# Third block's output projection: the stream's eight residual adds on GpSimd, placed between its weight splits, in place of VectorE

## The chip, the cores and the metric

The kernel runs on one core of a Trainium2 chip. The metric is the device time of one execution in microseconds (us). The core's engines are TensorE (PE, with its weight loads shown as PEld), VectorE (DVE), ScalarE (ACT), GpSimd (POOL) and SyncE (SP), which issues the weight loads from DRAM. Each engine runs its own instructions in program order, and they meet at semaphores.

## The reference, cut to what matters

Three blocks run one after the other on a stream of 1024 positions and 1024 features. The change lies in the third block, at the step that is marked:

```python
y = jnp.concatenate([rmsnorm_3(y_lru, out_norm_lru_g[l]),
                     rmsnorm_3(y_cc, out_norm_cc_g[l])], axis=-1)
h = h + y @ w_out[l].astype(y.dtype)                                  # this step

m = rmsnorm_3(h, norm_mlp_g[l]) @ w_mlp_up[l].astype(h.dtype)
h = h + jnp.square(jax.nn.relu(m)) @ w_mlp_down[l].astype(h.dtype)
```

## The kernel before

The stream `H3` lies in SBUF with features on the partitions, as eight tiles (index `b`) of 128 features x 1024 positions in float32. Every matrix product is made of three: each float32 operand is split into a high part and a low part (`whi`, `wlo` for weights, `xhi`, `xlo` for data), and PE multiplies high by high, high by low and low by high.

**Weights.** They come as slots of 16 tiles of 128x128. SP loads a slot into `RAW`, and GpSimd splits it (`split`, four pieces of 128x512, each a high part at L573 or L575 and a low part at L577) into one of two buffers. PE gives a buffer back when it starts the slot after it (`slot_used`), so GpSimd can be one slot ahead of PE. In a part of the third block ScalarE makes the high parts (`weights_high`), and GpSimd makes the low ones only (`split_low`, L585); the last slot made so is the second and last one of `out_3b`. The slot after it is the first of the MLP's up projection (`up_3_0`), the next one its second.

**The projection.** `w_out` is applied in two halves. The half over the recurrent branch (`out_3a`) has been added to the stream's old value by then, and lies in `HL3`, two tiles named `h3_low` (b 0 to 3) and `h3_high` (b 4 to 7). The half over the convolution branch, `out_3b`, is multiplied out by `feature_tiles` into PSUM, eight outputs in four "quads" of two; a quad's half of PSUM is used again two quads later. Its result needs a factor per position, `INVC` (`cc_inverse`). So for each of the eight outputs VectorE does two things: L2702 multiplies the PSUM result by `INVC` into `H3[b]` and frees its part of PSUM, and L2704 adds `HL3` to it and counts up `h3_done`.

**What follows.** After `h3_done` ScalarE squares the tile (`norm_square`, L302) for the sum of the next norm, and makes its high part with the norm's gain (`raw_high`, L342). VectorE adds up the squares (`norm_add`, L310) and makes the low part (`raw_low`, L346). These stand in one written order on each engine. On VectorE it is: multiply and add for b, then the norm's add and the low part for b-1, up to b = 4; at b = 5 the norm's adds for 4 and 5 and the low parts of 4 and 5; then multiply and add of 6 and 7, the low parts of 6 and 7, and the norm's adds of 6 and 7. On ScalarE it is square and high part of 0, 1, 2, 3, then squares of 4 and 5, high parts of 4 to 7, squares of 6 and 7.

The up projection's first output multiplies all eight tiles in order (k = 0 to 7) and waits before each one for its low part. The norm's factor itself is not needed then: its column sums are taken (L323) in the second output, and it is applied to the results.

Of the kernel before, what the change touches and what calls it, by code (L numbers as in the profile page):

```python
# [26 lines left out]
P = 128  # L27
D = 1024
KB = D // P
T = 1024  # L30
# [140 lines left out]
def build(nc, xT, memT, stream, params, wqkv, sgu, bias2, lru_w, metaT, outT, o_scr, h_scr, blocks=(1, 2, 3)):  # L171
    TL, WH = plan(blocks)
    NSLOT = len(TL) // TILES
    with ExitStack() as ctx:
# [15 lines left out]
        def L(name, n):  # L190
            return S(name), LATER[name][1] + n
# [5 lines left out]
        def S(name):  # L197
            if name in LATER:
                name = LATER[name][0]
            if name not in sems:  # L200
                sems[name] = ctx.enter_context(nc.semaphore(name))
            return sems[name]
# [3 lines left out]
        def at(name, offset, shape, dt=F32):  # L206
            return nc.alloc_sbuf_tensor_at(name, shape, dt, offset=base + offset)
# [12 lines left out]
        A = C + 8512  # L220
# [23 lines left out]
        def free(quad):  # L244
            return S(f"quad_free{quad % 2}")

        def freed(quad, ob, loop=None):

            return up(2 * (quad // 2) + ob + 1, loop)
# [4 lines left out]
        SHARED_3 = range(WH["vg_1"][0], WH["up_3_0"][0])  # L254
        SHARED = [*SHARED_M, *SHARED_3]
# [271 lines left out]
        if 1 in blocks:  # L527
            XS = at("x_in", A, [P, KB, T])
            MS = at("mem_in", A + 72704, [P, KB, MEM])

        def load_input(queue, b):
            queue.dma_start(XS[:, b:b + 2, :], xT[P * b:P * (b + 2), :].rearrange("(b p) t -> p b t", p=P))\
# [2 lines left out]
        def load_memory(queue, b):  # L535
            queue.dma_start(MS[:, b:b + 4, :], memT[P * b:P * (b + 4), :].rearrange("(b p) t -> p b t", p=P))\
                .then_inc(S("mem_moved"), 16)
# [25 lines left out]
        @block.gpsimd  # L563
        def _(pool):
            def split(r, loads, done, used):
                pool.wait_ge(raw_loaded[r], loads)
                if used is not None:
                    pool.wait_ge(slot_used, used)
                for piece in range(PIECES_W):
                    t = slice(TILES // PIECES_W * piece, TILES // PIECES_W * (piece + 1))  # L570
                    if piece == 0:
                        one = par("ones", 0, P).unsqueeze(1).to_broadcast([P, TILES // PIECES_W, P])
                        nc.gpsimd.tensor_tensor(WHI[:, r, t], RAW[:, r, t], one, ALU.mult).then_inc(hi_done, 1)  # L573
                    else:
                        nc.gpsimd.tensor_copy(WHI[:, r, t], RAW[:, r, t]).then_inc(hi_done, 1)  # L575
                    pool.wait_ge(hi_done, done + piece + 1)
                    ins = nc.gpsimd.tensor_tensor(WLO[:, r, t], RAW[:, r, t], WHI[:, r, t].bitcast(F32), ALU.subtract)  # L577
                ins.then_inc(split_done, 1)

            def split_low(s):  # L580
                r = s % 2
                for piece in range(PIECES_W):
                    t = slice(TILES // PIECES_W * piece, TILES // PIECES_W * (piece + 1))
                    pool.wait_ge(S("hi_by_act"), 2 * SHARED.index(s) + 2 * piece // PIECES_W + 1)
                    ins = nc.gpsimd.tensor_tensor(WLO[:, r, t], RAW[:, r, t], WHI[:, r, t].bitcast(F32), ALU.subtract)  # L585
                ins.then_inc(split_done, 1)

            def splits(first, end, fewer):
                if first % 2 and first < end:
                    split(1, 16 * (first // 2 + 1), PIECES_W * (first - fewer), first - 1)  # L590
                    first += 1
                if first // 2 < end // 2:
                    with pool.Fori(first // 2, end // 2) as i:
                        for r in range(2):
                            split(r, i * 16 + 16, i * (2 * PIECES_W) + PIECES_W * (r - fewer), i * 2 + (r - 1))
                if end % 2:
                    split(0, 16 * (end // 2 + 1), PIECES_W * (end - 1 - fewer), end - 2)

            for s in SHARED_M:
                split_low(s)  # L600
            pool.wait_ge(S("par_loaded"), 16)
            splits(SHARED_M.stop, SHARED_3.start, len(SHARED_M))
            for s in SHARED_3:
                split_low(s)
            splits(SHARED_3.stop, NSLOT, len(SHARED))


        if 1 in blocks:
# [50 lines left out]
            MXL = at("mem_lo", A + 65536, [P, KB, MEM], F32R)  # L659
            NRMM = norm_set("nm", lambda b: MS[:, b, :], MEM, lambda b: par("mem_norm_g", b), A + 81920, WH["mem_k"][1],  # L660
                            hi=lambda b: MXH[:, b, :], lo=lambda b: MXL[:, b, :])
# [887 lines left out]
        if 2 in blocks:  # L1549
# [15 lines left out]
                         at=NRM2["bank"] + 2 * BANK, columns=NRM2["bank"] + 2 * BANK, names=("e_sq", "e_add", "e_step", "e_x"))  # L1565
# [394 lines left out]
        if 3 in blocks:  # L1960
# [122 lines left out]
            SQ3 = at("squares_3", A, [P, 2, T])  # L2083
            DIAG3 = at("diag_3", A + 8192, [P, T])
            DIAG3M = at("diag_mean_3", A + 12288, [P, T])
            HL3 = [at("h3_low", A + 66624, [P, 4, T]), at("h3_high", A + 33536, [P, 4, T])]
            INVC = at("cc_inverse", A + 50240, [P, T])
            ROWS3 = at("rows_3", A + 83264, [64, T])
            THIRDS = ((0, 348), (348, 346), (694, 346))
# [1 line left out]
            MCOL = small("cc_mean_columns", [P, NT])  # L2091
            VCOL = small("cc_var_columns", [P, NT])
            RCOL = small("cc_root_columns", [P, NT])
            H3 = at("h3", A, [P, KB, T])
            NRMP = norm_set("n3p", lambda b: H3[:, b, :], T, lambda b: par("norm_mlp_g_3", b), A + 54336, WH["up_3_0"][1],
                            hi=lambda b: XHI[:, b, :], lo=lambda b: XLO[:, b, :], bank=2, spread_at=A + 81920)
            NRME = norm_set("n3o", lambda b: H3[:, b, :], T, lambda b: par("norm_final_g_3", b), A + 32768, 0,
# [75 lines left out]
        def pe_block3(pe):  # L2173
# [67 lines left out]
            def lru_half(o, between=None):  # L2241
# [22 lines left out]
                for a in (0, HALF):  # L2264
                    mm = nc.tensor.matmul(ps[:, c0 + a:c0 + a + HALF], IDENT, HL3[o // 4][:, o % 4, a:a + HALF],
                                          start=False, stop=True)
# [41 lines left out]
        def act_block3(act):  # L2308
# [130 lines left out]
            act.wait_ge(S("l_scan"), 4)  # L2439
            act.dma_start(HL3[0][:, :, :], h_blocks[:, 0:4, :]).then_inc(S("h3_loaded0"), 16)  # L2440
            act.wait_ge(S("cc_conv"), 2 * (CCK - 1))
# [18 lines left out]
            act.wait_ge(*L("l_lo", 4))  # L2460
            act.dma_start(HL3[1][:, :, :], h_blocks[:, 4:8, :]).then_inc(S("h3_loaded1"), 16)

# [70 lines left out]
        def dve_block3(dve):  # L2533
# [165 lines left out]
            for b in range(KB):  # L2699
                q = WH["out_3b"][1] + b // 2  # L2700
                dve.wait_ge(quad_ready, q + 1)
                nc.vector.tensor_tensor(H3[:, b, :], half(q, b % 2), INVC[:, :], ALU.mult).then_inc(free(q), 1)  # L2702
                dve.wait_ge(free(q), freed(q, b % 2))
                nc.vector.tensor_tensor(H3[:, b, :], H3[:, b, :], HL3[b // 4][:, b % 4, :], ALU.add).then_inc(S("h3_done"), 1)  # L2704
                if 1 <= b < 6:
                    norm_add(dve, NRMP, b - 1)
                if 1 <= b < 5:
                    raw_low(dve, NRMP, b - 1)
                if b == 5:
                    norm_add(dve, NRMP, 5)  # L2710
                    raw_low(dve, NRMP, 4)
                    raw_low(dve, NRMP, 5)
# [116 lines left out]
```

## Time and profile before

| | before |
|---|---|
| median of 3 runs | 3512.65 us (3509.48 to 3513.63) |
| the profiled execution | 3508.49 us, its span 3506.7 us |
| PE busy | 3337.4 us, 95% |
| DVE busy | 1362.1 us, 39% |
| POOL busy | 1194.7 us, 34% |
| ACT busy | 760.3 us, 22% |
| chain that ended last | PE 87%, DVE 8%, ACT 3% |

PE is busy nearly all of the time, so the kernel's time moves only where PE waits, or where it does its work at a lower clock. The stretch that matters here lies between 2736 and 2801 us from the start of the span: `out_3b`, and the first outputs of the up projection behind it. The views used are the page's lines on busy time and on the chain, the chain of waits in that stretch, and the timelines of single engines in it. In a timeline a row gives the start, the duration, the engine, the line and operation, what is written and read, and in brackets the engine's idle time before it and what ended that.

### The profile page before, as it was taken

The page shows a single profiled execution, that of the slowest core. Times are in us where ns is not written, and L with a number is a line of the kernel's source. Part 1 is how long each engine was busy: PE and PEld are TensorE (multiplying, and loading weights), DVE is VectorE, ACT ScalarE, POOL GpSimd, SP SyncE. Part 2 cuts the span into 40 slices and gives each one's busy share as a digit, 9 for nine tenths or more (in the row PEclk, how much of TensorE's full clock was granted, in tenths as well). Part 3 has the DMA queues.
Part 4 walks back from the last instruction along what each step waited for, and adds up shares of the span by engine and source line. Part 5 has one row for each costly group of instructions (what it writes and reads, how often), then busy time and mean ns, then how long its engine had stood idle before and what let it go on. Part 6 is the DMA issues. An engine that isn't in the chain of part 4 may idle for free.

```text
span 3506.7 us, 37515 instructions
## 1 busy us (share of the span) xinstructions
PE 3337.4 (95%) x15576; PEld 2680.3 (76%) x15576; DVE 1362.1 (39%) x1653; ACT 760.3 (22%) x1108; POOL 1194.7 (34%) x992
## 2 busy tenths in 40 slices
PE   7999989999898999999999999998998999999997
PEld 6577767888785788888888888887965788888886
DVE  6264073331505402233331111238997652222223
ACT  4220164221205401112100000023542310000001
POOL 5212300354330233344443433342321454444441
PEclk9989999999898999999999999998998999999998
DMA  4111100021210011121111111112111111111111
GB/s 186 37 43 43 49 1 25 25 89 65 105 48 13 24 48 55 43 97 48 48 49 48 48 48 48 48 48 78 37 60 48 36 49 48 48 48 48 48 48 48
DMA packets 32333, 181.72 MB, mean 52 GB/s; under 512 B 3920, under 2 KB 4944, under 8 KB 15312
## 3 DMA queue, kind: packets, MB, share of 16 engines
q1 hardware_dynamic: 19936, 139.99, 11.2%
q10 hardware_dynamic: 12272, 39.89, 3.0%
q8 instruction: 99, 1.62, 0.2%
q14 instruction: 26, 0.21, 0.0%
HBM read 164.15 MB, written 15.73 MB: 51 GB/s over the span
## 4 chain that ended last, share of the span: by engine, by line
PE 87%; DVE 8%; ACT 3%; issue 1%; POOL 1%; DMA 0%; DVEq 0%; ACTq 0%; SPq 0%; POOLq 0%
PE ps L451 50%; PE ps L485 17%; PE ps L2134 5%; PE ps L516 4%; DVE c_out L2584 2%; PE ps L1635 1%; PE ps L860 1%; PE ps L1651 1%; PE ps L2156 1%; PE ps L733 1%; PE ps L2210 1%; DVE p L1830 1%; PE ps L1621 1%; PE ps L742 1%; PE ps L877 1%
## 5 line engine op out<-in xcount | busy, mean ns | idle before, releaser
L573 POOL TENSOR_TENSOR whi<-raw,par 128x512 fp32r<-128x512 f32 x116 | 127.8, 1102 | 1923.7 <-PE ps L451 1398.3
L577 POOL TENSOR_TENSOR wlo<-raw,whi 128x512 fp32r<-128x512 f32 x464 | 687.5, 1482 | 37.0
L451 PE MATMUL ps<-xhi,whi 128*128 128x512 f32 x2016 | 628.0, 393 | 11.8 <-DVE xlo L346 4.3
L451 PE MATMUL ps<-xlo,whi 128*128 128x512 f32 x2016 | 624.1, 391 | 0.0
L451 PE MATMUL ps<-xhi,wlo 128*128 128x512 f32 x2016 | 622.7, 390 | 0.0
L451 PEld LDWEIGHTS ps<-xhi,whi 128*128 128x128 f32 x2016 | 376.9, 188 | 95.5 <-issue 5.3
L451 PEld LDWEIGHTS ps<-xhi,wlo 128*128 128x128 f32 x2016 | 379.7, 188 | 81.0
L451 PEld LDWEIGHTS ps<-xlo,whi 128*128 128x128 f32 x2016 | 380.0, 189 | 80.3
L575 POOL CAST whi<-raw 128x512 fp32r<-128x512 f32 x348 | 287.8, 827 | 0.0
L485 PE MATMUL ps<-hidden_hi,whi 128*128 128x512 f32 x864 | 268.6, 392 | 0.4 <-DVE hidden_lo L1491 0.4
L485 PE MATMUL ps<-hidden_lo,whi 128*128 128x512 f32 x864 | 268.9, 393 | 0.0
L485 PE MATMUL ps<-hidden_hi,wlo 128*128 128x512 f32 x864 | 267.1, 390 | 0.0
L1506 DVE TENSOR_TENSOR h<-h,ps 128x1024 f32<-128x1024 f32 x112 | 132.3, 1217 | 337.7 <-PE ps L485 337.7
L1453 ACT ACTIVATE ff_act<-ps 128x1024 f32<-128x1024 f32 x46 | 47.3, 1028 | 977.3 <-PE ps L451 977.3
L585 POOL TENSOR_TENSOR wlo<-raw,whi 128x512 fp32r<-128x512 f32 x60 | 110.7, 1874 | 290.0 <-ACT whi L262 290.0
L485 PEld LDWEIGHTS ps<-hidden_hi,wlo 128*128 128x128 f32 x864 | 162.2, 188 | 36.7
L485 PEld LDWEIGHTS ps<-hidden_lo,whi 128*128 128x128 f32 x864 | 162.3, 188 | 35.7
L485 PEld LDWEIGHTS ps<-hidden_hi,whi 128*128 128x128 f32 x864 | 161.3, 188 | 36.4 <-issue 1.7
L2584 DVE SCALAR_TENSOR_TENSOR c_out<-c_in,par,c_out 128x1024 f32<-128x1024 f32 x120 | 179.2, 1495 | 4.9 <-ACT c_out L2356 1.4
L1482 DVE TENSOR_TENSOR ff_tmp<-ff_act,ps 128x1024 f32<-128x1024 f32 x18 | 22.0, 1221 | 328.0 <-ACT ff_act L1453 328.0
L1487 DVE TENSOR_TENSOR ff_tmp<-ff_act 128x1024 f32<-128x1024 f32 x32 | 41.7, 1303 | 216.6 <-ACT ff_act L1453 216.5
L1491 DVE TENSOR_TENSOR hidden_lo<-ff_tmp,hidden_hi 128x1024 fp32r<-128x1024 f32 x54 | 90.6, 1678 | 63.9 <-ACT hidden_hi L1456 63.9
(487 smaller groups left out, 4577.3 us busy)
## 6 DMA issues: line engine op xcount, KB each, us to landing
raw<-stream SPq DMA_DIRECT2D x131, 1024.0 KB, 4.7
x_again<-xT ACTq DMA_DIRECT2D x4, 1024.0 KB, 8.0
h_scr<-x_again ACTq DMA_DIRECT2D x4, 1024.0 KB, 4.4
h<-h_scr ACTq DMA_DIRECT2D x1, 4096.0 KB, 15.4
h_scr<-h ACTq DMA_DIRECT2D x4, 1024.0 KB, 4.6
outT<-h ACTq DMA_DIRECT2D x8, 512.0 KB, 3.0
bias<-bias ACTq DMA_DIRECT2D x1, 2560.0 KB, 9.0
x_in<-xT ACTq DMA_DIRECT2D x2, 1024.0 KB, 17.5
```

The lines of the kernel that those rows point to most:

```text
L451: mm = nc.tensor.matmul(ps[:, c0 + c:c0 + c + width], w, x(k, a, width), start=(n == 0 and m == 0), stop=(n == len(ks) - 1 and m == 2))
L485: mm = nc.tensor.matmul(ps[:, c0 + c:c0 + c + HALF], w, x(k, a, HALF), start=(k == 0 and m == 0), stop=(k == n - 1 and m == 2))
L516: mm = nc.tensor.matmul(ps[:, c:c + BANK], x(k, P * tt, P), w, start=(k == 0 and m == 0), stop=(k == KB - 1 and m == 2))
L573: nc.gpsimd.tensor_tensor(WHI[:, r, t], RAW[:, r, t], one, ALU.mult).then_inc(hi_done, 1)
L575: nc.gpsimd.tensor_copy(WHI[:, r, t], RAW[:, r, t]).then_inc(hi_done, 1)
L577: ins = nc.gpsimd.tensor_tensor(WLO[:, r, t], RAW[:, r, t], WHI[:, r, t].bitcast(F32), ALU.subtract)
L585: ins = nc.gpsimd.tensor_tensor(WLO[:, r, t], RAW[:, r, t], WHI[:, r, t].bitcast(F32), ALU.subtract)
L1453: nc.scalar.activation(FA[:, j % 2, :], half(q, 0), ACT.Silu if k == "f2" else ACT.Relu)\
L1491: nc.vector.tensor_tensor(HL[:, j, :], FT[:, j % 2, :], HH[:, j, :].bitcast(F32), ALU.subtract)\
L1506: nc.vector.tensor_tensor(stream_tile[:, b, :], stream_tile[:, b, :], half(q, b % 2), ALU.add).then_inc(free(q), 1)
L2134: mm = nc.tensor.matmul(ps[:, c0 + BANK * i:c0 + BANK * i + width], w, x(k, a, width), start=(k == 0 and m == 0), stop=(k == KB - 1 and m ...
L2584: nc.vector.scalar_tensor_tensor(CCO[:, b, :], CC[:, b, META + k:META + k + T], par("cc_conv_w_3", 4 * k + b), CCO[:, b, :], ALU.mult, ALU ...
```

## The change

VectorE keeps the eight multiplications by `INVC` and loses the eight adds of `HL3`. GpSimd gets them, as a function `residual(b)`: it waits for VectorE's multiplication of b, for the load of `HL3` and for ScalarE's last write to it, adds 128x1024 values and counts up `h3_done`. In GpSimd's order the adds of b = 0, 1, 2 stand behind the last `split_low`, then comes the split of the up projection's first slot, then the adds of b = 3 to 7, then the remaining splits.

```diff
+            def residual(b):
+
+                q = WH["out_3b"][1] + b // 2
+                pool.wait_ge(free(q), freed(q, b % 2))
+                pool.wait_ge(*L(f"h3_loaded{b // 4}", 16))
+                pool.wait_ge(*L("lh_kept", 8))
+                nc.gpsimd.tensor_tensor(H3[:, b, :], H3[:, b, :], HL3[b // 4][:, b % 4, :], ALU.add).then_inc(S("h3_done"), 1)
+
+            s = SHARED_3.stop
+            for b in range(3):
+                residual(b)
+            splits(s, s + 1, len(SHARED))
+            for b in range(3, KB):
+                residual(b)
+            splits(s + 1, NSLOT, len(SHARED))
-            splits(SHARED_3.stop, NSLOT, len(SHARED))
...
                 nc.vector.tensor_tensor(H3[:, b, :], half(q, b % 2), INVC[:, :], ALU.mult).then_inc(free(q), 1)
-                dve.wait_ge(free(q), freed(q, b % 2))
-                nc.vector.tensor_tensor(H3[:, b, :], H3[:, b, :], HL3[b // 4][:, b % 4, :], ALU.add).then_inc(S("h3_done"), 1)
```

GpSimd's order behind the last `split_low` (40 subtractions in a row), before. `raw` is the loaded slot, `num_ready` stands for `lh_kept`, `x_again0` and `x_again1` for the loads of `HL3`, `quad_free` for VectorE's multiplication:

```order
53 L585 TENSOR_TENSOR wlo<-raw,whi 128x512 [waits hi_by_act] x40
54 L573 TENSOR_TENSOR whi<-raw,par 128x512 [waits slot_used,raw_loaded1]
55 L577 TENSOR_TENSOR wlo<-raw,whi 128x512 [waits hi_done]
56 L575 CAST whi<-raw 128x512
57 L577 TENSOR_TENSOR wlo<-raw,whi 128x512 [waits hi_done]
58 L575 CAST whi<-raw 128x512
```

and in the changed kernel, where `h_61` is the stream `H3`:

```order
53 L587 TENSOR_TENSOR wlo<-raw,whi 128x512 [waits hi_by_act] x40
54 L614 TENSOR_TENSOR h_61<-h_61,h_low 128x1024 [waits num_ready,x_again0,quad_free0] x2
55 L614 TENSOR_TENSOR h_61<-h_61,h_low 128x1024 [waits num_ready,x_again0,quad_free1]
56 L575 TENSOR_TENSOR whi<-raw,par 128x512 [waits slot_used,raw_loaded1]
...
63 L579 TENSOR_TENSOR wlo<-raw,whi 128x512 [waits hi_done]
64 L614 TENSOR_TENSOR h_61<-h_61,h_low 128x1024 [waits num_ready,x_again0,quad_free1]
65 L614 TENSOR_TENSOR h_61<-h_61,h_high 128x1024 [waits num_ready,x_again1,quad_free0] x2
66 L614 TENSOR_TENSOR h_61<-h_61,h_high 128x1024 [waits num_ready,x_again1,quad_free1] x2
```

The eight adds stand in front of and behind the split of the first up slot, and the next split stands behind them all.

VectorE's order from the multiplication of b = 5 on, before:

```order
1132 L2702 TENSOR_TENSOR h3_535<-ps,cc_inverse_529 128x1024 [waits quad_ready]
1133 L2704 TENSOR_TENSOR h3_535<-h3_535,h3_high_528 128x1024 [waits quad_free0]
1134 L310 TENSOR_TENSOR n3p_acc_537<-n3p_acc_537,n3p_sq_536 128x1024 [waits norm_add,norm_sq] x2
1135 L346 SCALAR_TENSOR_TENSOR xlo_53<-h3_535,par_54,xhi_52 128x1024 [waits norm_hi] x2
1136 L2702 TENSOR_TENSOR h3_535<-ps,cc_inverse_529 128x1024 [waits quad_ready]
1137 L2704 TENSOR_TENSOR h3_535<-h3_535,h3_high_528 128x1024 [waits quad_free1]
1138 L2702 TENSOR_TENSOR h3_535<-ps,cc_inverse_529 128x1024 [waits quad_ready]
1139 L2704 TENSOR_TENSOR h3_535<-h3_535,h3_high_528 128x1024 [waits quad_free1]
1140 L346 SCALAR_TENSOR_TENSOR xlo_53<-h3_535,par_54,xhi_52 128x1024 [waits norm_hi] x2
```

and in the changed kernel:

```order
1127 L2717 TENSOR_TENSOR h3_61<-ps,cc_inverse_562 128x1024 [waits quad_ready]
1128 L310 TENSOR_TENSOR n3p_acc_569<-n3p_acc_569,n3p_sq_568 128x1024 [waits norm_add,norm_sq] x2
1129 L346 SCALAR_TENSOR_TENSOR xlo_53<-h3_61,par_54,xhi_52 128x1024 [waits norm_hi] x2
1130 L2717 TENSOR_TENSOR h3_61<-ps,cc_inverse_562 128x1024 [waits quad_ready] x2
1131 L346 SCALAR_TENSOR_TENSOR xlo_53<-h3_61,par_54,xhi_52 128x1024 [waits norm_hi] x2
```

Only the adds are gone; the multiplications of 6 and 7 still stand behind the norm's add of 5 and the low parts of 4 and 5.

## Rows read from the trace of the kernel before

**Rows 1.** The page: busy time of each engine, and the chain by engine.

```profile
PE 3337.4 (95%) x15576; PEld 2680.3 (76%) x15576; DVE 1362.1 (39%) x1653; ACT 760.3 (22%) x1108; POOL 1194.7 (34%) x992
PE 87%; DVE 8%; ACT 3%; issue 1%; POOL 1%; DMA 0%; DVEq 0%; ACTq 0%; SPq 0%; POOLq 0%
```

**Rows 2.** The chain of waits, 2736 to 2830: start, us, engine and line.

```profile
2736.29 10.95 PE ps L451 x48
...
2747.26 1.24 DVE h L2702
...
2779.80 1.56 DVE xlo L346
2781.36 0.04 issue
2781.40 6.02 PE ps L451 x18
```

**Rows 3.** Timeline of PE, the end of six steps and the next two.

```profile
2768.82 0.62 PE L451 MATMUL ps<-xhi,whi 128*128 128x512 f32 x2
...
2776.52 0.61 PE L451 MATMUL ps<-xhi,wlo 128*128 128x512 f32 x2
2781.40 0.85 PE L451 MATMUL ps<-xhi,whi 128*128 128x512 f32 x2 [4.26 <-DVE xlo L346]
...
2783.75 1.10 PE L451 MATMUL ps<-xhi,whi 128*128 128x512 f32 x2
...
2787.26 1.84 PE L323 MATMUL ps<-par,n3p_acc 128*128 128x1 f32 x16
```

**Rows 4.** Timeline of DVE, 2737 to 2784.

```profile
2737.39 1.23 DVE L2702 TENSOR_TENSOR h<-ps,cc_inverse 128x1024 f32<-128x1024 f32 x1 [4.29 <-ACT cc_inverse L2499]
2738.65 2.11 DVE L2704 TENSOR_TENSOR h<-h,h_low 128x1024 f32<-128x1024 f32 x1
...
2744.18 2.31 DVE L346 SCALAR_TENSOR_TENSOR xlo<-h,par,xhi 128x1024 fp32r<-128x1024 f32 x1
2747.26 1.23 DVE L2702 TENSOR_TENSOR h<-ps,cc_inverse 128x1024 f32<-128x1024 f32 x1 [0.77 <-PE ps L451]
2748.52 1.25 DVE L2704 TENSOR_TENSOR h<-h,h_low 128x1024 f32<-128x1024 f32 x1
...
2762.44 1.22 DVE L310 TENSOR_TENSOR n3p_acc<-n3p_acc,n3p_sq 128x1024 f32<-128x1024 f32 x1
2763.58 1.28 DVE L346 SCALAR_TENSOR_TENSOR xlo<-h,par,xhi 128x1024 fp32r<-128x1024 f32 x1
2764.77 1.22 DVE L2702 TENSOR_TENSOR h<-ps,cc_inverse 128x1024 f32<-128x1024 f32 x1
...
2779.72 3.85 DVE L346 SCALAR_TENSOR_TENSOR xlo<-h,par,xhi 128x1024 fp32r<-128x1024 f32 x2
```

**Rows 5.** Timeline of ACT, square and high part of tile 0.

```profile
2740.79 1.06 ACT L302 ACTIVATE n3p_acc<-h 128x1024 f32<-128x1024 f32 x1 [1.54 <-DVE h L2704]
2741.75 1.14 ACT L342 ACTIVATE xhi<-h,par 128x1024 fp32r<-128x1024 f32 x1
```

**Rows 6.** Timeline of POOL, 2738 to 2801.

```profile
2738.38 7.04 POOL L585 TENSOR_TENSOR wlo<-raw,whi 128x512 fp32r<-128x512 f32 x4 [70.11 <-ACT whi L262]
2747.59 1.09 POOL L573 TENSOR_TENSOR whi<-raw,par 128x512 fp32r<-128x512 f32 x1 [2.18 <-PE ps L451]
...
2759.13 2.15 POOL L577 TENSOR_TENSOR wlo<-raw,whi 128x512 fp32r<-128x512 f32 x1
2769.29 1.38 POOL L573 TENSOR_TENSOR whi<-raw,par 128x512 fp32r<-128x512 f32 x1 [8.01 <-PE ps L451]
...
2800.93 1.16 POOL L573 TENSOR_TENSOR whi<-raw,par 128x512 fp32r<-128x512 f32 x1 [18.44 <-PE ps L451]
```

**Rows 7.** Timeline of POOL from 3304 on, a split in the MLP.

```profile
3304.41 1.09 POOL L573 TENSOR_TENSOR whi<-raw,par 128x512 fp32r<-128x512 f32 x1 [13.65 <-PE ps L451]
3305.58 1.29 POOL L577 TENSOR_TENSOR wlo<-raw,whi 128x512 fp32r<-128x512 f32 x1
3306.82 0.61 POOL L575 CAST whi<-raw 128x512 fp32r<-128x512 f32 x1
...
3311.36 1.28 POOL L577 TENSOR_TENSOR wlo<-raw,whi 128x512 fp32r<-128x512 f32 x1
```

## What was predicted before the changed kernel ran

> **What bounds the kernel now.** I read the page first: PE is busy 95% of the span and carries 87% of the chain [rows 1], so only what delays PE counts. The chain of waits in the stretch of the projection comes second. It leaves PE at 2747.26, when the third and fourth outputs are multiplied out, goes through VectorE's list of work without a break, and comes back to PE at 2781.40 [rows 2]. The timeline of PE shows the price: the up projection's first output starts at 2768.82, does six of its eight steps by 2777.1, and idles 4.26 us for the low part of tile 6 [rows 3]. Then the two steps from 2781.40 to 2785.88 take 4.5 us, where six took 8.3 us, so 1.37 us each: another 1.7 us are lost to slow matmuls after the gap. Taking this stall away whole would give 4.3 + 1.7 = 6 us. The event to follow is the low part of tile 7, done at 2783.57 [rows 4]; PE starts its eighth step at 2783.75 [rows 3].
>
> **What things take.** VectorE's multiplication takes 1.23 us, a two-input operation without disturbance 1.2 [rows 4]; ScalarE's square 1.06 and high part 1.14 us [rows 5]. VectorE's operations with two inputs in SBUF are stretched where GpSimd works: the add at 2738.65 took 2.11 and the low part at 2744.18 took 2.31 us, against 1.25 and 1.28 at other places [rows 4], and GpSimd's subtraction 2.15 against 1.29 us [rows 6, 7]. The stretch of 1.1 us is one instruction of the other engine: they take turns. The multiplication reads PSUM and one SBUF tile, and isn't stretched.
>
> GpSimd has no 128x1024 operation in the trace. The nearest is its subtraction of 128x512, 1.29 us, with the next instruction 1.24 us behind it [rows 7]. Twice the spacing is 2.48 us; a fixed part that is paid once rather than twice makes it less, and turn-taking makes it more. I take 2.45 us. The bounds are 2.2 (0.25 us of fixed part) and, if an add is disturbed for its whole length as the worst subtractions are, 2 x 2.15 = 4.3 us [rows 6].
>
> The Trainium skill (GPSIMD Engine Reference, section 3.1) gives 4497 ns for an add of 2048 columns against 2293 ns on VectorE. Half of it would be an estimate of 2.25 us, and the sum below would come out at +5 in place of +7 us. The subtraction of 512 columns, 1.29 us, is a little above a quarter of it (1.12), so the trace bears it out with a fixed part of some 0.15 us.
>
> **The walk through the changed kernel.** Adds on GpSimd are A0 to A7.
>
> The last `split_low` holds GpSimd from 2738.38 for 7.04 us, with three turns lost to VectorE's adds and a low part [rows 6]; the adds are gone and the low part comes later, so four spacings of 1.24 end it at 2743.3. Before, add 0 was done at 2740.8. Now A0 ends at 2745.7 and A1 at 2748.1. Square and high part of tile 0 end at 2747.9, its low part at 2749.2, and only behind it stands the multiplication of tile 2, done 2750.3. The norm's add 1 takes the turn to 2751.4, so A2 ends at 2753.8. The split of the first up slot, which began at 2747.59 [rows 6], begins behind A2: 6.2 us late. A split by itself takes 8.2 us (3304.41 to 3312.64) [rows 7]; this one took 13.7 (2747.59 to 2761.28) [rows 6]. Now only the low parts of 1 and 2 and the norm's add 2 take turns with it, 1.0 us each, so it ends near 2765.1, 3.8 us later than now; PE doesn't want it before 2768.82.
>
> But tile 3 has to wait for it: A3 runs to 2767.5, A4 to 2769.9. On VectorE the norm's add 3 and low part 3 (high part 3 at 2769.7) stand ahead of multiplication 5, which ends at 2773.3 in place of 2766 [rows 4]. PE needs that PSUM at 2768.82 for its first up output, so it starts 4.5 us late; six steps end by 2781.6, and even with 1.7 us for slow matmuls by 2783.3. A5 loses a turn to the norm's add 4 and ends at 2776.7. Square 5, high part 4 and high part 5 on ScalarE (3.2 us) end at 2779.9, low parts 4 and 5 at 2781.4, and behind them multiplication 6 at 2782.6. A6 ends at 2785.1, A7 at 2787.5, high part 7 at 2788.7. Low part 6 has waited for A7's turn and ends at 2788.7; GpSimd's next split takes a turn of 1.1, and low part 7 ends at 2790.8. That is 7.2 us behind the 2783.57 of now. Walking the kernel of before in the same way ends 0.1 to 0.7 us later than its trace, so I take 7 us.
>
> The gap of PE ahead of its seventh step grows to some 5 us, at 1.7 us of slow matmuls as now. The norm's add 7 ends at 2794.7; PE wants it for the column sums at the same time, 3.5 us after its eighth step began, as now (2783.75 to 2787.26) [rows 3], so it adds nothing. The second up slot, split from 2769.29 on before [rows 6], is split from 2787.5, with two low parts and two adds in its way, to 2799.6; PE took it up at 2800.9, where GpSimd's next split was released [rows 6], and now does at 2807.9. That cover of 8 us hides it. The load of slots by SP hangs on splits and stays ahead. The rest of the MLP is PE work and moves as a whole.
>
> Sum: eight VectorE adds gone, which would be worth up to 6 us at PE; in their place eight adds of twice the length, one of which stands behind a split of 11 us, and hand-overs from VectorE to GpSimd to ScalarE and back that VectorE's own order makes serial. +7 us. Each 0.1 us of GpSimd's add moves it by 0.75 us, as seven to eight adds lie on this path: 2.2 gives +5, 2.6 gives +8. The profiled execution was 3508.5 and would be 3515.5; it lies 4.2 us below the median of the runs. The median, 3512.65, plus 7 gives **3519.6 us**.
>
> **The rule of turns.** The rows show turns of 1.1 us only. The Trainium skill (SBUF — State Buffer, section Who interferes with whom) says that a VectorE instruction with two SBUF inputs and a GpSimd instruction that reads SBUF exclude each other for the whole instruction, whoever comes first. By that rule an add of 2.45 us makes VectorE wait up to 2.3 us, which the walk has in it at low parts 1 and 6 and at add 3. If a long add let VectorE in, those waits and what they push would go, and the walk would end about 4 us sooner, at +3. No row has so long an instruction on GpSimd.
>
> **Rivals.**
> 1. *Nearly hidden.* The wide add is at its lower bound, or VectorE isn't held for the whole of it: +2 to +5 us. For it: PE's gap was 4.3 us, so the path has been off PE's own work for long only from tile 4 on. Against it: the walk's turns all have a pattern in rows 4 and 6. Chance 0.27.
> 2. *GpSimd's add is dearer*, 3 us or more, through turns lost within it or slower dispatch: at 3 us +11, at 4.3 us +21 or so, where the second up slot's split also has its cover used up to the last microsecond. It decides from 2.6 us on. Chance 0.17.
> 3. *Faster.* VectorE's list was the bound from 2747 to 2781, and eight of its operations, 1.25 to 2.11 us each [rows 4], 10 to 17 us together, leave it. If GpSimd worked beside it freely, PE would find all low parts in time: at most 6 us less, 3506.6. The mechanism needs an add at 1.3 us or less, or no turns at all; then the walk ends level with now. Against it stands that multiplications 5 and 6 each wait on VectorE behind work that needs the add before. Chance 0.05.
> 4. *The change doesn't do what it says:* VectorE isn't relieved, as it stands idle where it was busy. This is in the forecast, and has no time of its own.
>
> **How the numbers follow.** Forecast, +5 to +10 us, 0.51; rival 1, 0.27; rival 2, 0.17; rival 3, 0.05. A measurement of this kernel tells 0.2%, 7 us, from no change. The forecast's own case lies astride that bound and gives 0.33 to slower and 0.18 to the same; rival 1 is the same, rival 2 slower, rival 3 faster. That makes faster 0.04, same 0.46, slower 0.50. The range leaves out the far part of rival 2 and rival 3: +1.4 to +14 us, 3514 to 3526.5.
>
> **What would show it.** In the timeline of GpSimd: adds near 2.45 us, and add 3 beginning some 11 us after add 2 ended. In VectorE's: idle times ended by ScalarE where there were none, and multiplications 5 and 6 about 7 us later. On PE: a new wait of about 4 us ahead of the first up output, ended by VectorE's multiplication, and a wait of about 5 us ahead of the seventh step. The prediction is wrong if the split of the first up slot ends before 2762, if the adds take under 2 or over 2.8 us, or if PE's column sums start less than 3 us later than 2787.3.

## The result, and the profile after

| | before | after |
|---|---|---|
| median | 3510.12 us (20 runs, 3507.37 to 3515.4) | 3516.4 us (20 runs, 3514.12 to 3522.09) |
| ratio to before | | 1.0018, 95% interval 1.0012 to 1.0024 |
| span of the profiled execution | 3506.7 us | 3514.6 us |
| DVE busy | 1362.1 us | 1350.1 us |
| POOL busy | 1194.7 us | 1210.7 us |

The changed kernel is 6.3 us slower by the medians. That is just inside the 0.2% that was set as the limit of no change, and the interval of the ratio, 4.2 to 8.4 us, lies wholly above zero. The first three runs of the kernel before had a median 2.5 us above that of all its 20 runs, so 2.5 of the 3.2 us between the forecast of 3519.6 and the measured 3516.4 lie in the starting point.

The page of the changed kernel, busy time and the chain by engine (compare [rows 1]):

```profile
PE 3340.9 (95%) x15576; PEld 2681.2 (76%) x15576; DVE 1350.1 (38%) x1645; ACT 761.9 (22%) x1108; POOL 1210.7 (34%) x1000
PE 86%; DVE 8%; ACT 3%; issue 2%; POOL 1%; DMA 0%; DVEq 0%; ACTq 0%; SPq 0%; POOLq 0%
```

Times inside the stretch can be compared from one common point, ScalarE's copy of `INVC` ahead of VectorE's first multiplication. It starts at 2736.33 us before and at 2737.13 after; the 0.8 us between them arose earlier, in code that is the same. GpSimd in the changed kernel (compare [rows 6]; L614 is the add, L575 to L579 the split):

```profile
2739.19 5.05 POOL L587 TENSOR_TENSOR wlo<-raw,whi 128x512 fp32r<-128x512 f32 x4 [71.61 <-ACT whi L262]
2744.19 4.79 POOL L614 TENSOR_TENSOR h<-h,h_low 128x1024 f32<-128x1024 f32 x2
2751.28 3.33 POOL L614 TENSOR_TENSOR h<-h,h_low 128x1024 f32<-128x1024 f32 x1 [2.29 <-DVE h L2717]
2754.56 2.08 POOL L575 TENSOR_TENSOR whi<-raw,par 128x512 fp32r<-128x512 f32 x1
...
2765.84 2.42 POOL L614 TENSOR_TENSOR h<-h,h_low 128x1024 f32<-128x1024 f32 x1
2768.22 2.38 POOL L614 TENSOR_TENSOR h<-h,h_high 128x1024 f32<-128x1024 f32 x1
2774.09 3.29 POOL L614 TENSOR_TENSOR h<-h,h_high 128x1024 f32<-128x1024 f32 x1 [3.49 <-DVE h L2717]
2783.33 4.69 POOL L614 TENSOR_TENSOR h<-h,h_high 128x1024 f32<-128x1024 f32 x2 [5.95 <-DVE h L2717]
2787.97 2.08 POOL L575 TENSOR_TENSOR whi<-raw,par 128x512 fp32r<-128x512 f32 x1
...
2808.73 1.16 POOL L575 TENSOR_TENSOR whi<-raw,par 128x512 fp32r<-128x512 f32 x1 [7.86 <-PE ps L451]
```

An undisturbed add takes 2.4 us. Add 3 starts at 2765.84, 11.2 us after add 2 ended, since the split stands between them. Three times GpSimd waits for VectorE's multiplication, 2.29, 3.49 and 5.95 us, and all three times VectorE's order has the multiplication behind work that needs an earlier add. VectorE, in the same stretch (compare [rows 4]):

```profile
2738.19 2.36 DVE L2717 TENSOR_TENSOR h<-ps,cc_inverse 128x1024 f32<-128x1024 f32 x2 [4.30 <-ACT cc_inverse L2514]
2748.77 1.30 DVE L346 SCALAR_TENSOR_TENSOR xlo<-h,par,xhi 128x1024 fp32r<-128x1024 f32 x1 [8.22 <-ACT xhi L342]
...
2752.26 3.43 DVE L346 SCALAR_TENSOR_TENSOR xlo<-h,par,xhi 128x1024 fp32r<-128x1024 f32 x1
...
2769.39 2.29 DVE L310 TENSOR_TENSOR n3p_acc<-n3p_acc,n3p_sq 128x1024 f32<-128x1024 f32 x1 [8.07 <-ACT n3p_sq L302]
...
2772.80 1.21 DVE L2717 TENSOR_TENSOR h<-ps,cc_inverse 128x1024 f32<-128x1024 f32 x1
...
2786.93 4.20 DVE L346 SCALAR_TENSOR_TENSOR xlo<-h,par,xhi 128x1024 fp32r<-128x1024 f32 x2 [2.55 <-ACT xhi L342]
```

VectorE, which hardly stood still before, is idle for 8.22 and 8.07 us, and its last low part ends at 2791.13, 54.0 us after the common point where it was 47.2 (2783.57 less 2736.33). The wait on PE, which is what counts (compare [rows 3]; the second row shown here is the seventh step, the third the column sums):

```profile
2774.07 1.22 PE L451 MATMUL ps<-xhi,whi 128*128 128x512 f32 x2 [4.28 <-DVE h L2717]
...
2789.15 0.89 PE L451 MATMUL ps<-xhi,whi 128*128 128x512 f32 x2 [4.20 <-DVE xlo L346]
...
2794.98 1.93 PE L323 MATMUL ps<-par,n3p_acc 128*128 128x1 f32 x16
```

There is a new wait of 4.28 us ahead of the first up output, and the old one ahead of the seventh step is still 4.20 us long. Behind each wait the matmuls are slow for a while: a pair takes 1.05 us where 0.62 is usual, and the clock granted to PE is 0.50 of full speed (1.2 GHz) from 2775 to 2778 us and from 2790 to 2792, where it is 1.00 (2.4 GHz) from 2784 to 2788. Before, it was 0.50 from 2782 to 2784, behind the one wait.

### The profile page after: what moved, and what is told of

Same layout as the page of the kernel before. It is cut to its first block, busy times and chain, and to the rows that moved or that the text cites. A ratio compares the mean times of both kernels' runs of the same rounds, so it can differ in the third digit from the quotient of the medians.

```text
span 3514.6 us, 37523 instructions
## 1 busy us (share of the span) xinstructions
PE 3340.9 (95%) x15576; PEld 2681.2 (76%) x15576; DVE 1350.1 (38%) x1645; ACT 761.9 (22%) x1108; POOL 1210.7 (34%) x1000
## 4 chain that ended last, share of the span: by engine, by line
PE 86%; DVE 8%; ACT 3%; issue 2%; POOL 1%; DMA 0%; DVEq 0%; ACTq 0%; SPq 0%; POOLq 0%
PE ps L451 50%; PE ps L485 17%; PE ps L2149 5%; PE ps L516 4%; DVE c_out L2599 2%; PE ps L877 1%; PE ps L1652 1%; PE ps L1668 1%; PE ps L750 1%; PE ps L2225 1%; DVE p L1847 1%; PE ps L759 1%; PE ps L1638 1%; POOL h L614 1%; PE ps L894 1%
## 5 line engine op out<-in xcount | busy, mean ns | idle before, releaser
L575 POOL TENSOR_TENSOR whi<-raw,par 128x512 fp32r<-128x512 f32 x116 | 129.6, 1117 | 1903.9 <-PE ps L451 1375.0
L579 POOL TENSOR_TENSOR wlo<-raw,whi 128x512 fp32r<-128x512 f32 x464 | 685.0, 1476 | 36.9
```

## The experiments

Beside the medians, the table gives a local figure: the time from the common point to PE's start on the second up slot, which is where GpSimd's following split is released (2800.93 in [rows 6]). It is read in the one profiled execution and is free of what happens elsewhere in the 3500 us. For the kernel before it is 64.6 us. How much it varies from one execution to the next wasn't measured; two pairs of kernels that should differ little there, before and e9, after and e7, agree within 0.1 us.

| kernel | median, us | before in the same comparison | ratio, 95% interval | local, us | against before |
|---|---|---|---|---|---|
| after | 3516.4 | 3510.12 | 1.0018 (1.0012 to 1.0024) | 71.6 | +7.0 |
| e1 all adds ahead of the split | 3530.26 | 3510.01 | 1.0059 (1.0042 to 1.0076) | 85.5 | +20.9 |
| e2 half of each add | 3510.14 | 3510.01 | 1.0002 (0.9993 to 1.0012) | 65.1 | +0.5 |
| e3 each add in two halves | 3517.24 | 3510.01 | 1.0021 (1.0011 to 1.0031) | 72.4 | +7.8 |
| e4 adds 3 to 7 on GpSimd | 3511.25 | 3510.01 | 1.0007 (0.9998 to 1.0017) | 67.5 | +2.9 |
| e5 split held back, before | 3506.86 | 3509.57 | 0.9994 (0.9985 to 1.0003) | 61.7 | -2.9 |
| e6 no adds | 3505.55 | 3509.57 | 0.9987 (0.9978 to 0.9996) | 58.4 | -6.2 |
| e7 split held back, after | 3516.3 | 3509.57 | 1.0019 (1.001 to 1.0029) | 71.5 | +6.9 |
| e8 held back, and reordered | 3504.23 | 3509.64 | 0.9983 (0.9974 to 0.9992) | 59.5 | -5.1 |
| e9 reordered only | 3510.05 | 3509.64 | 1.0001 (0.9991 to 1.001) | 64.5 | -0.1 |
| e10 held back until add 7 | 3505.09 | 3509.64 | 0.9987 (0.9977 to 0.9996) | 59.7 | -4.9 |

The theory was that of the prediction: the adds' length on the path, and the split that stands between add 2 and add 3 (theory A). Its main rival was that the hand-overs between three engines cost the time, whatever is handed over (theory B).

### e1: all eight adds ahead of the first up slot's split

```diff
-            for b in range(3):
+            for b in range(KB):
                 residual(b)
-            splits(s, s + 1, len(SHARED))
-            for b in range(3, KB):
-                residual(b)
-            splits(s + 1, NSLOT, len(SHARED))
+            splits(s, NSLOT, len(SHARED))
```

> All eight adds stand on GpSimd in front of the first up slot's split, nothing is left out. Theory A (the path runs through eight wide adds, and the split between them holds adds 3 to 7 back by 11 us): without the split in between, the low part of tile 7 is done about as early as in the kernel before, within 2 us of it (some 46 us after VectorE's first multiplication, where the changed kernel has 53). But PE then waits for the split itself, which ends near 28 us after the adds began to end: PE's first up output starts some 24 us later than before, and the time is 3530 us, 20 us over the kernel before. Theory B (the hand-overs between the three engines cost the time, wherever the split stands): the low part of tile 7 stays 6 to 7 us late and the time is 3536 us, 26 over the kernel before.

Measured: 3530.26 us. GpSimd's timeline, the last adds and the split that PE now waits for:

```profile
2756.74 3.31 POOL L614 TENSOR_TENSOR h<-h,h_low 128x1024 f32<-128x1024 f32 x1 [2.30 <-DVE h L2714]
...
2777.16 4.64 POOL L614 TENSOR_TENSOR h<-h,h_high 128x1024 f32<-128x1024 f32 x2 [5.95 <-DVE h L2714]
2781.76 2.07 POOL L575 TENSOR_TENSOR whi<-raw,par 128x512 fp32r<-128x512 f32 x1
```

VectorE's last two low parts in its timeline:

```profile
2780.72 4.20 DVE L346 SCALAR_TENSOR_TENSOR xlo<-h,par,xhi 128x1024 fp32r<-128x1024 f32 x2 [2.50 <-ACT xhi L342]
```

PE's timeline, where the first step of the up projection now waits and not the seventh:

```profile
2793.68 1.19 PE L451 MATMUL ps<-xhi,whi 128*128 128x512 f32 x2 [24.05 <-issue]
```

Add 3 starts 2.3 us after add 2 ended and not 11.2. The last low part ends at 2784.92, 48.0 us after the common point (2736.97), only 0.7 us later than before. So eight wide adds on GpSimd with all their hand-overs, with no split among them, end the low parts under a microsecond later than the eight adds on VectorE did; with the split among them it was 6.8 us. Theory B would have left 6 to 7 us here, and falls as the reason why the changed kernel is slower than the one before. That doesn't make the hand-overs free: the 0.7 us is what is left when the relief of VectorE is taken off, and e6 below gives that relief. PE pays elsewhere, 24.05 us for the split: the trace names no releaser, but the split's last instruction ends at 2793.58, 0.1 us before PE starts. Its column sums start 20.9 us later than before (71.8 against 50.9 us from the common point). The split can't go behind the adds; it has to go between them or ahead of them.

### e2: each add does only half of its columns

```diff
-                nc.gpsimd.tensor_tensor(H3[:, b, :], H3[:, b, :], HL3[b // 4][:, b % 4, :], ALU.add).then_inc(S("h3_done"), 1)
+                nc.gpsimd.tensor_tensor(H3[:, b, 0:HALF], H3[:, b, 0:HALF], HL3[b // 4][:, b % 4, 0:HALF], ALU.add).then_inc(S("h3_done"), 1)
```

> The changed kernel, but each of the eight adds does only the first 512 of 1024 columns; the other half is left out. An add should take 1.29 us and not 2.4. Theory A (length of the adds, 0.75 us of time for each 0.1 us of an add): the time is that of the kernel before within 1.5 us, 3510 us. Theory B (hand-overs, the same number of them): the time stays at 3514 us or above, at least two thirds of the 6.3 us that the change cost.

Measured: 3510.14 us, the time of the kernel before. The same number of adds in the same places, with the same hand-overs, costs no more than VectorE's own adds did when an add takes 1.30 us. Adds 3 and 4, and the row from which the local figure is read (the common point is 2737.92):

```profile
2764.38 1.30 POOL L614 TENSOR_TENSOR h<-h,h_low 128x512 f32<-128x512 f32 x1
2765.64 1.30 POOL L614 TENSOR_TENSOR h<-h,h_high 128x512 f32<-128x512 f32 x1
...
2803.06 1.16 POOL L575 TENSOR_TENSOR whi<-raw,par 128x512 fp32r<-128x512 f32 x1 [10.07 <-PE ps L451]
```

1.1 us less for each add took 6.5 us off the local figure, 0.59 us for each 0.1 us of an add, where the prediction had 0.75. Together with e1: for the low parts to come some 7 us later than before, both the wide adds and the split in the middle are needed. With only one of the two, the low parts come 0.7 us (e1) and 0.3 us (e2) later than before.

### e3: each add as two adds of 512 columns

```diff
-                nc.gpsimd.tensor_tensor(H3[:, b, :], H3[:, b, :], HL3[b // 4][:, b % 4, :], ALU.add).then_inc(S("h3_done"), 1)
+                nc.gpsimd.tensor_tensor(H3[:, b, 0:HALF], H3[:, b, 0:HALF], HL3[b // 4][:, b % 4, 0:HALF], ALU.add)
+                nc.gpsimd.tensor_tensor(H3[:, b, HALF:T], H3[:, b, HALF:T], HL3[b // 4][:, b % 4, HALF:T], ALU.add).then_inc(S("h3_done"), 1)
```

> The changed kernel, but each add is made as two adds of 512 columns, one right behind the other, so GpSimd can be made to give way in the middle. Theory A (the sum of the adds' lengths counts, long turns hardly): the same time as the changed kernel within 1.5 us, 3516 us, low parts 1 and 6 of VectorE stretched by 1.2 us rather than 2.2. Rival C (it is the long turn of 2.4 us, during which VectorE stands still, that costs): at least 3 us less than the changed kernel, 3513 us.

Measured: 3517.24 us, 0.8 us over the changed kernel, and 0.8 in the local figure. VectorE's low part 1 is stretched less, as expected:

```profile
2750.44 2.32 DVE L346 SCALAR_TENSOR_TENSOR xlo<-h,par,xhi 128x1024 fp32r<-128x1024 f32 x1
```

2.32 us stand against 3.43 in the changed kernel. For low part 6 the expectation missed: low parts 6 and 7 took 4.34 us together, against 4.20. What VectorE gains at low part 1 GpSimd loses in the next turn (one half of add 2 took 2.28 us), and two halves start 2.49 us before the next add where a whole one started 2.38 us before it. Cutting the long turn brings nothing, so long turns as such aren't what costs; rival C falls.

### e4: adds 0 to 2 back on VectorE, adds 3 to 7 on GpSimd behind the split

```diff
-            for b in range(3):
-                residual(b)
             splits(s, s + 1, len(SHARED))
             for b in range(3, KB):
                 residual(b)
...
+                if b < 3:
+                    dve.wait_ge(free(q), freed(q, b % 2))
+                    nc.vector.tensor_tensor(H3[:, b, :], H3[:, b, :], HL3[b // 4][:, b % 4, :], ALU.add).then_inc(S("h3_done"), 1)
```

> Adds 0, 1 and 2 back on VectorE, adds 3 to 7 on GpSimd behind the first up slot's split, which starts as early as in the kernel before. Theory A: the split ends at about 24 us after VectorE's first multiplication, add 3 follows at once, and what is left of the cost is five wide adds: 2 to 3 us over the kernel before, 3512.5 us. Theory B (hand-overs): five eighths of 6.3 us, 3514 us. Rival D (the cost lies in the first three adds alone, which hold up the split): no cost, 3510 us.

Measured: 3511.25 us. The first split starts at 2747.70 and add 3 at 2760.51, 24.1 us after the common point (2736.43) and not 28.7:

```profile
2747.70 1.09 POOL L575 TENSOR_TENSOR whi<-raw,par 128x512 fp32r<-128x512 f32 x1 [2.17 <-PE ps L451]
...
2760.51 2.41 POOL L614 TENSOR_TENSOR h<-h,h_low 128x1024 f32<-128x1024 f32 x1
```

The local figure is 2.9 us over the kernel before, theory A's 2 to 3. By the medians it is 1.2 us, with an interval that holds anything from a gain of 0.7 to a loss of 6 us, so the medians alone would not tell it from rival D. The local figure does, 4.1 us below the changed kernel and 2.9 above the one before: some 4 of the 7 us come with the first three adds on GpSimd, which hold the up slot's split back (it starts 11.3 us after the common point here, and 17.4 in the changed kernel), and 3 with the five wide adds behind it. The edit also puts three adds back on VectorE and takes away their hand-overs, and how the 4 us divide between that and the later split isn't shown.

### e6: what taking the adds off VectorE could bring at most

The kernel before, without the adds; ScalarE waits for the multiplications.

```diff
-                act.wait_ge(*L("h3_done", b + 1))
+                act.wait_ge(free(WH["out_3b"][1] + b // 2), freed(WH["out_3b"][1] + b // 2, b % 2))
                 norm_square(act, NRMP, b)
...
-                act.wait_ge(*L("h3_done", b + 1))
+                act.wait_ge(free(WH["out_3b"][1] + b // 2), freed(WH["out_3b"][1] + b // 2, b % 2))
...
-                dve.wait_ge(free(q), freed(q, b % 2))
-                nc.vector.tensor_tensor(H3[:, b, :], H3[:, b, :], HL3[b // 4][:, b % 4, :], ALU.add).then_inc(S("h3_done"), 1)
```

> The kernel before without the eight adds of the stream (they are left out; ScalarE waits for the multiplications instead). This is the most that taking the adds off VectorE could bring. Theory A: low part 7 is done 8 us earlier, PE's gap ahead of the seventh step is gone and its slow matmuls too: 5 to 6 us under the kernel before, 3504.5 us. Rival F (another engine's work is late next, ScalarE's squares or GpSimd's split): less than 3 us, 3507.5 us or more.

Measured: 3505.55 us, 4.0 us under before (interval of the ratio: 1.4 to 7.7 us), and 6.2 us in the local figure; PE has no gap left between 2765 and 2802, and its granted clock is 1.00 throughout. VectorE's last two low parts, and GpSimd's row for the local figure (the common point is 2743.15):

```profile
2778.29 2.93 DVE L346 SCALAR_TENSOR_TENSOR xlo<-h,par,xhi 128x1024 fp32r<-128x1024 f32 x2
```

```profile
2801.52 1.15 POOL L573 TENSOR_TENSOR whi<-raw,par 128x512 fp32r<-128x512 f32 x1 [13.45 <-PE ps L451]
```

So 6 us is all there was to win by taking the adds off VectorE, the size given in the prediction for the whole stall. Rival F falls by the local figure; the interval of the medians alone reaches into its range of less than 3 us.

This kernel is also the right one to hold the hand-overs against. Its last low part ends 38.1 us after the common point, 9.2 us sooner than before. In e1 it ends at 48.0 and in e2 at 47.5, so eight adds on GpSimd, with their hand-overs, end the low parts 9.9 and 9.5 us later than no adds at all; at PE, e2 stands 6.7 us above e6 in the local figure. The change wins the relief and pays for the adds and hand-overs; it comes out level in e2, and 7 us short in the changed kernel. How much of the price is the hand-overs' own, no run tells.

### e5, e7, e10: hold the second up slot's split back

The prediction's rule of turns suggests another way to the same 6 us: VectorE's last adds and low parts are stretched by the split of the second up slot, and that split isn't needed before 2800. So GpSimd waits with it. e5 is the kernel before with this one wait, e7 the changed kernel with it:

```diff
-            splits(SHARED_3.stop, NSLOT, len(SHARED))
+            splits(SHARED_3.stop, SHARED_3.stop + 1, len(SHARED))
+            pool.wait_ge(S("norm_lo"), 56)
+            splits(SHARED_3.stop + 1, NSLOT, len(SHARED))
```

(`norm_lo` reaches 56 with the low part of tile 7.) In e10 the wait is for the norm's add 7 instead:

```diff
+            pool.wait_ge(S("norm_add"), 42)
```

> The kernel before with one more wait and nothing else: GpSimd begins the split of the second up slot only when VectorE has made the low part of tile 7. Theory A (turns with GpSimd's split stretch VectorE's last adds and low parts; the split has time): VectorE's work from the norm's add 4 to low part 7 is free of turns and ends 3 to 4 us earlier, PE's gap of 4.3 us ahead of its seventh step shrinks to 1 us or less and with it some of the slow matmuls behind it; the split ends near 8 us after low part 7, 6 us before PE takes it up. Time 3506 us, 3 to 5 us under the kernel before. Rival E (turns shift work about but VectorE waits for ScalarE anyway, or the later split makes PE wait): no gain, 3510 us, or a loss.

> The changed kernel with the same wait as in the held split: GpSimd begins the second up slot's split only behind low part 7. Theory A: the split's first instruction no longer takes a turn ahead of low part 7, nor do the following ones in the norm's adds 6 and 7: 1 to 2 us less than the changed kernel, 3515 us, since all other turns are with the adds themselves and with the first up slot's split. Rival G (most of the cost of the change is turns with the second split): 4 us or more less, 3512 us.

> The kernel before with the second up slot's split held until the norm's add 7 is done, no other edit. Theory A: as the split held until low part 7 (3506.9 us, 2.7 us under the kernel before), with the norm's add 7 no longer stretched by 0.7 us: 3506.5 us, PE's gap ahead of its seventh step 1.0 us, the gap ahead of the column sums gone. Rival E (nothing or a loss): 3510 us.

Measured: e5 3506.86 us, 2.7 under before, with an interval that just reaches no change; e10 3505.09 us, 4.6 under, interval 1.4 to 8.1 us; e7 3516.3 us, no gain on the changed kernel. VectorE's end in e5, unstretched (compare the 3.85 us for the same two in [rows 4]):

```profile
2779.45 2.58 DVE L346 SCALAR_TENSOR_TENSOR xlo<-h,par,xhi 128x1024 fp32r<-128x1024 f32 x2
```

It ends 43.1 us after the common point (2738.95), 4.2 us sooner than before, and PE's gap shrinks from 4.26 to 1.01 us. The held split ends 11.0 us after low part 7 and not 8, as it takes turns with the norm's adds, and is still done 7.5 us before PE takes it up.

```profile
2780.78 0.74 PE L451 MATMUL ps<-xhi,whi 128*128 128x512 f32 x2 [1.01 <-DVE xlo L346]
```

Not all of it came through in e5: a stretch of slow matmuls appears after the column sums, in the timeline 1.06 us for a pair in place of 0.62, and in the table by stretches (PE's granted clock is the figure behind POOL's busy time) at 0.59 between 2788 and 2792:

```profile
2788.00:2792.00 4.00, 4.00 (x12) 3.12 (x12) 1.32 (x1) 0.00 (x0) 3.84 (x5) 0.59 0.00 0
```

In e10 the same stretch stands at full clock, and the local figure is 2.0 us better than e5's:

```profile
2788.00:2792.00 4.00, 4.00 (x18) 3.09 (x17) 1.28 (x1) 0.00 (x0) 3.84 (x4) 1.00 0.00 0
```

From its seventh step to the column sums PE takes 4.47 us in e5 and 4.24 in e10, so the two kernels differ by 0.2 us of waiting there, and there is one profile of each; what tips the clock isn't settled here, nor whether e10's lead over e5 by the medians, 1.8 us, is more than noise.

e7 missed its 1 to 2 us. Two low parts took 3.58 in place of 4.20 us, but PE was at its seventh step with slow matmuls for all of that time, and its column sums start 57.8 us after the common point, where they started 57.9 after it in the changed kernel. The saving had slack to fall into. It also says that turns with the second split are no part of the change's cost (rival G).

### e8, e9: a version faster than both

e8 adds to e10 that the norm's add 5 moves behind low part 7, and that PE takes the column sums and the spread one step later; e9 has these two edits without the hold.

```diff
                 if b == 5:
-                    norm_add(dve, NRMP, 5)
                     raw_low(dve, NRMP, 4)
                     raw_low(dve, NRMP, 5)
             raw_low(dve, NRMP, KB - 2)
             raw_low(dve, NRMP, KB - 1)
+            norm_add(dve, NRMP, 5)
...
-            before = N and {(1, 1): lambda: norm_columns(pe, N), (1, 4): lambda: norm_spread(pe, N),
+            before = N and {(1, 2): lambda: norm_columns(pe, N), (1, 5): lambda: norm_spread(pe, N),
```

> The kernel before with the second up slot's split held until the norm's add 7 is done, the norm's add 5 moved behind low part 7, and PE's column sums and spread one step later in the second up output. Theory A: no gap of PE is left ahead of the seventh step and none ahead of the column sums (the held split alone left 1.0 and 0.3 us, and a stretch of slow matmuls behind them): from ScalarE's cc_inverse to the end of the second up output about 6 us shorter than in the kernel before, 3504 us. Rival E (the slow stretch comes back wherever the 128x1 column sums stand): 3506.5 us, as with the held split alone.

> The same without holding the split back: only the norm's add 5 behind low part 7 and the column sums one step later. Theory A (turns with the second split are what holds VectorE up, not its order): low part 6 comes at most 1.2 us sooner, as the turns with the split stay; time within 2 us of the kernel before, 3509 us. Rival H (the order is the cost): 3 us or more under the kernel before.

Measured: e8 3504.23 us, 5.4 us under before (interval 2.8 to 9.1 us) and some 12 us under the changed kernel, as each was measured against the kernel before; e9 3510.05 us, no gain. The order alone does nothing, the hold alone nearly all: e8 lies 0.9 us under e10 by the medians and 0.2 in the local figure, which is too little to tell from nothing. PE's seventh step and column sums in e8:

```profile
2780.88 0.74 PE L451 MATMUL ps<-xhi,whi 128*128 128x512 f32 x2 [0.81 <-DVE xlo L346]
2786.49 1.84 PE L323 MATMUL ps<-par,n3p_acc 128*128 128x1 f32 x16
```

The first instructions of the held split and of the one behind it, in GpSimd's timeline:

```profile
2786.26 1.09 POOL L573 TENSOR_TENSOR whi<-raw,par 128x512 fp32r<-128x512 f32 x1 [22.04 <-DVE n3p_acc L310]
...
2798.76 1.09 POOL L573 TENSOR_TENSOR whi<-raw,par 128x512 fp32r<-128x512 f32 x1 [3.45 <-PE ps L451]
```

The gap ahead of the seventh step is 0.81 us, where theory A expected none: VectorE now waits for ScalarE's high part 4 where the norm's add 5 stood (1.04 us), so the move bought 0.2 us. No slow matmuls follow it, which speaks against rival E. The split begins 22 us after the one before and still ends 3.45 us before PE takes it up.

## Why the prediction was right

**The bound.** PE's wait for the low parts, ended by VectorE, was the right place. e6 shows that it was worth 6.2 us, where 6 had been worked out from the gap and the slow matmuls behind it.

**The add's length.** Taken as 2.45 us from twice the spacing of the 512-column subtractions [rows 7]; measured 2.38 to 2.42 us. The Trainium skill's figure (GPSIMD Engine Reference, section 3.1) had led to 2.25 us by halving; the trace is 0.15 us above it, as the 512-column instructions were a little above a quarter of it.

**The walk.** Its steps against the trace, each from the common point of its profile (2736.33 for the walk, 2737.13 for the trace):

| event | walk | trace |
|---|---|---|
| add 3 starts | 28.8 | 28.7 |
| multiplication 5 ends | 37.0 | 36.9 |
| PE starts the first up output | 37.0 | 36.9 |
| add 6 starts | 46.3 | 46.2 |
| add 7 ends | 51.2 | 50.9 |
| low part 7 ends | 54.5 | 54.0 |
| PE's column sums start | 58.4 | 57.9 |

The new wait of PE was put at 4.5 us and is 4.28, the old one at 5 and is 4.20. The cover of the second up slot's split was put at 8 us and is 7.86. The sum was +7; the local figure is +7.0 and the medians give +6.3. One term was too small without harm: 1.7 us had been put down for slow matmuls behind the new wait, and they cost 2.5 (the two steps from 2774.07 to 2779.34 took 5.3 us, where two steps at full clock take 2.7). PE waits for the low parts behind them anyway, and its second wait is that much shorter.

**Turns.** The walk let VectorE wait for a whole add, on a rule that no row had shown for so long an instruction. The changed kernel shows it: low part 1 took 3.43 us, 1.28 of its own and 2.15 of waiting for add 2, as far as the rows tell. The Trainium skill (SBUF — State Buffer, section Who interferes with whom) says that the two exclude each other for the whole instruction; by this rule, the trace agrees.

**What was off.** The sensitivity, 0.75 us for each 0.1 us of an add, is 0.59 over the range that e2 covers. The prediction had counted seven to eight adds on the path; with adds 1.1 us shorter, e2's add 3 starts 2.2 us sooner than the changed kernel's, add 5 4.4, add 6 5.5 and low part 6 6.6 us, and low part 7 ends 6.5 us sooner. That is the length of six adds. Add 1 isn't on the path, as it ends at 2748.98 while the multiplication of tile 2 waits for low part 0, whose high part ended at 2748.73; and the turn that add 7 takes ahead of low part 6 is taken in e2 by the split behind it. The closing remark of the sum named the hand-overs beside the lengths as a cause; e1 and e2 show that, with shorter adds or without the split among them, they and the adds together cost what the relief of VectorE brings, and their own share stays open. The chance of "slower by over 0.2%" was 0.50 and that of "the same" 0.46; with a ratio of 1.0018 it was the second. The forecast of 7 us lay on the bound itself, so which side the measurement fell on was luck; and the median of 3519.6 was 3.2 us high mostly because its starting point, three runs, was.

**Rivals.** Nearly hidden (+2 to +5 us), a dearer add, and faster did not come. The interval of the medians, 4.2 to 8.4 us, still reaches the upper end of the first; the local figure of +7.0 and its two conditions, an add at 2.2 us or a VectorE that isn't held for the whole of it, decide against it. The premise of "faster" was right in one half: VectorE's list was the bound, and the kernel before gains 4.6 to 5.4 us where that list is shortened by its turns and not by its adds (e10, e8).

## What to carry to other kernels

An engine that is idle a third of the time isn't free: what is moved to it lands among its own jobs, in its order, and a long job between two of the moved pieces can decide the matter: here the low parts came 6.8 us late with the split between the adds, and 0.7 without it. Walk the whole loop of engines with each one's written order before moving work, and count the moved operation at the new engine's length. Where two engines take turns at SBUF, first look whether the background job can be held back until the critical list is through; here one wait in e10 brought 4.9 us in the local figure, where leaving the eight adds out altogether brought 6.2 and moving them cost 7.0.

## What the runs showed of the hardware

In these traces turns between VectorE and GpSimd alternate one instruction at a time, and a waiting instruction's row grows by about what is left of the other's: 3.33 us for an add of 2.4 with one turn lost, 3.43 us for a low part of 1.28. Where GpSimd waited for nothing, each of its rows in the changed kernel ended within 0.1 us of the start of the next, so here they could be used as durations.

The profiled executions differ before the changed stretch by more than some of the effects: the common point lies at 2736.33 us before and at 2743.15 in e6, with the same code ahead of it. The cause wasn't looked for; differences of a few microseconds were therefore read from a point near the change.
